# The MLP's falling products with weights stationary: tokens move, sums are kept by features and turned at the end

## Reference

```
hid = square(relu(rms_norm(x, g_pre_mlp) @ w_up))      # w_up   1024 x 4096
y   = x + rms_norm(hid @ w_down, g_post_mlp)           # w_down 4096 x 1024
rms_norm(v, g) = v * rsqrt(mean(v*v over the features) + 1e-6) * g
```

## Time and profile before

| | |
|---|---|
| median of 3 runs | 2000.29 us (1996.58 to 2002.13) |
| the profiled execution, its own time | 2001.27 us |
| its span, first to last instruction | 1999.5 us |
| mean granted TensorE clock | 0.978 of full |
| busy: PE / PEld / DVE / ACT / POOL | 1911.2 / 1720.5 / 1154.8 / 712.1 / 584.6 us |
| first matmul of the MLP / last one ends | 1187.5 / 1976.7 us |
| rising products, 2304 matmuls, start to start | 23.91 us a chunk |
| falling products, 1728 matmuls, start to start | 25.27 us a chunk |

### The profile page before, as it was taken

One profiled execution on the slowest core, in us unless ns is written; L12 is line 12 of the kernel. 1 busy time (PEld: TensorE's weight loads), 2 busy tenths in 40 slices (PEclk: granted clock), 3 DMA queues, 4 the chain that ended last, 5 costly groups with the idle time before them and its releaser, 6 DMA issues. The chain is left out here.

```text
span 1999.5 us, 31095 instructions
## 1 busy us (share of the span) xinstructions
PE 1911.2 (96%) x11132; PEld 1720.5 (86%) x11132; DVE 1154.8 (58%) x2651; ACT 712.1 (36%) x1420; POOL 584.6 (29%) x445
## 2 busy tenths in 40 slices
PE   5999999999999999999988979999999999999995
PEld 5889999877779999999987858888888888888884
DVE  5249999998645666676755653333333333333337
ACT  4335544233334555555644331122211221112212
POOL 2316544234223334343311012222222222222224
PEclk9999999999988999999998989999999999999998
DMA  5423333333446444443214321111111111111204
GB/s 169 130 67 91 94 98 90 87 100 97 103 121 140 97 97 97 97 97 86 66 27 158 121 95 43 43 43 46 42 42 42 43 46 42 42 42 42 63 0 158
DMA packets 180393, 160.18 MB, mean 80 GB/s; under 512 B 101472, under 2 KB 148432, under 8 KB 180288
## 3 DMA queue, kind: packets, MB, share of 16 engines
q1 hardware_dynamic: 166144, 140.32, 25.0%
q10 hardware_dynamic: 14144, 18.49, 4.0%
HBM read 120.63 MB, written 39.27 MB: 80 GB/s over the span
## 5 line engine op out<-in xcount | busy, mean ns | idle before, releaser
L2142 PE MATMUL ps<-x2T_hi,weights 128*128 128x362 f32 (+1 forms) x1536 | 383.5, 329 | 5.3 <-DVE weights L2108 5.3
L2160 PE MATMUL ps<-weights,hid_hi 128*128 128x512 f32 (+1 forms) x1152 | 363.0, 396 | 0.0
L2142 PEld LDWEIGHTS ps<-x2T_hi,weights 128*128 128x128 f32 x1536 | 273.7, 189 | 7.0 <-DVE weights L2108 5.5
L2093 DVE TENSOR_TENSOR total<-total,ps 128x512 f32<-128x512 f32 (+1 forms) x270 | 184.8, 686 | 164.3 <-PE ps L2160 163.4
L2160 PEld LDWEIGHTS ps<-weights,hid_hi 128*128 128x128 f32 (+1 forms) x1152 | 209.6, 182 | 57.1
L2142 PE MATMUL ps<-x2T_lo,weights 128*128 128x362 f32 (+1 forms) x768 | 253.0, 329 | 0.0
L976 PE MATMUL ps<-xT_hi,w 128*128 128x362 f32 (+1 forms) x960 | 246.1, 331 | 1.6 <-PEq L160 1.6
L2078 DVE TENSOR_TENSOR hidden<-hidden 128x362 f32<-128x362 f32 (+1 forms) x96 | 51.6, 537 | 311.3 <-ACT hidden L2051 311.3
L2160 PE MATMUL ps<-weights,hid_lo 128*128 128x512 f32 (+1 forms) x576 | 228.1, 396 | 0.0
L2011 POOL TENSOR_TENSOR weights<-down_raw,weights 128x512 fp32r<-128x512 f32 x64 | 82.8, 1294 | 419.9 <-ACT weights L2042 419.9
L951 DVE MATCH_REPLACE8 score<-top,score 128x1024 f32<-128x1024 f32 (+5 forms) x208 | 198.8, 961 | 0.0
(11 more groups left out here) (187 smaller groups left out, 3225.5 us busy)
## 6 DMA issues: line engine op xcount, KB each, us to landing
q_raw<-q_scr SPq DMA_DIRECT2D x80, 256.0 KB, 5.1
w_raw<-in_w_in ACTq DMA_DIRECT2D x64, 256.0 KB, 3.0
up_raw<-in_w_up SPq DMA_DIRECT2D x64, 256.0 KB, 2.8
down_raw<-in_w_down SPq DMA_DIRECT2D x64, 256.0 KB, 2.6
gates<-gate_scr SPq DMA_DIRECT2D x34, 256.0 KB, 4.6
x_in<-in_x_prompt SPq DMA_DIRECT2D x16, 512.0 KB, 4.8
gate_scr<-stage SPq DMA_DIRECT2D x32, 256.0 KB, 3.1
q_scr<-stage SPq DMA_DIRECT2D x40, 181.0 KB, 3.1
```

Of the source, the lines that this page charges most:

```text
L2093: dve.tensor_tensor(out, out, ps[:r, UP_BANKS + g % DOWN_BANKS, :], ALU.add).then_inc(added, 1)
L2142: last = pe.matmul(ps[:, g % UP_BANKS, 0:n], a[:, k, fs], b, start=(k == 0 and i == 0), stop=(k == KT - 1 and i == 2))
L2160: last = pe.matmul(ps[:r, UP_BANKS + g % DOWN_BANKS, :], a, b[:, f, cols], start=(f == 0 and i == 0), stop=(f == FT - 1 and i == 2))
```

## The change

The falling products swap their operands. A 128 x 128 slice of `w_down` is stationary, and the hidden values of a token block (364 or 362 tokens) move. The groups are (feature tile o of 8, token block b of 3), block by block: 24 a chunk, of 6 matmuls. The result, and so `total`, has output features on the partitions: `[P, KT, N_QUERY]`. VectorE adds 24 pieces of 364 or 362 columns a chunk. The norm runs over the features and the output is stored by tokens, so each token tile is transposed at the end: 8 transposes of 128 x 128 into two PSUM banks (`turn_total`). ScalarE squares and VectorE scales out of these banks, into `y`, three buffers, where GpSimd adds the residual and SP stores from.

The last chunk is now written out after the loop. Tiles 0 to 3 are transposed during it, after groups 10, 14, 18 and 22, into banks 0 and 1, and scaled by VectorE after its additions 11, 15, 19 and 23; tiles 4 to 8 after the last group (tiles 4 and 8 in banks 0 and 1, tiles 5, 6, 7 in banks 2 to 7). A tile that reuses banks waits for the scaling of the tile before in them; a scaling from tile 3 on waits for the store of three tiles before.

```diff
@@ -1916,7 +1916,9 @@
...
     UP_GROUPS = [(f, t0, n) for f in range(FT) for t0, n in TOK_BLOCKS]
-    DOWN_GROUPS = [(t, half) for t in range(TILES) for half in range(2)]
+    DOWN_GROUPS = [(o, b) for b in range(len(TOK_BLOCKS)) for o in range(KT)]
+    BLOCK_END = [t0 + n for t0, n in TOK_BLOCKS]
+    PER_BLOCK = KT
     N_UP, N_DOWN = len(UP_GROUPS), len(DOWN_GROUPS)
@@ -1932,7 +1934,8 @@
...
         hid_lo = sb("hid_lo", [P, FT, N_QUERY], F32R)
-        total = sb("total", [P, TILES, D])
+        total = sb("total", [P, KT, N_QUERY])
+        y = sb("y", [P, 3, D])
         x1_in = sb("x1_in", [P, 2, D])
@@ -1946,12 +1949,29 @@
...
         sq_done, std_ready, rstd_ready, refined = sem("p5_sq_done"), sem("p5_std_ready"), sem("p5_rstd_ready"), sem("p5_refined")
-        scaled, y_ready, y_stored = sem("p5_scaled"), sem("p5_y_ready"), sem("p5_y_stored")
+        y_turned = sem("p5_y_turned")
+        scaled, y_ready, y_stored = sem("p5_scaled"), sem("p5_y_ready"), [sem(f"p5_y_stored{i}") for i in range(3)]
...
         FIRST_BY_DVE = range(1, KT, 2)
+        def whole_after(t):
+            return PER_BLOCK * (1 + min(b for b, end in enumerate(BLOCK_END) if t * P + tile_rows(t) <= end))
+        LAST_BANKS = [0 if whole_after(t) < N_DOWN or t == SAMPLE_TILE else 2 * (t % 4) for t in range(TILES)]
+        TURNED_AT = [PER_BLOCK + 2, PER_BLOCK + 6, 2 * PER_BLOCK + 2, 2 * PER_BLOCK + 6] + [N_DOWN] * (TILES - 4)
+        SCALED_AT = [at + 1 if at < N_DOWN else at for at in TURNED_AT]
+        def y_banks(t):
+            return ps[:tile_rows(t), LAST_BANKS[t]:LAST_BANKS[t] + 2, :].rearrange("p b n -> p (b n)")
+        def banks_used_before(t):
+            return max((s for s in range(t) if LAST_BANKS[s] == LAST_BANKS[t]), default=None)
@@ -1959,7 +1979,7 @@
...
                 dst = y_prompt[0, toks(t), :] if t < SAMPLE_TILE else y_sample[0]
-                sp.dma_start(dst, total[:r, t, :]).then_inc(y_stored, 16)
+                sp.dma_start(dst, y[:r, t % 3, :]).then_inc(y_stored[t % 3], 16)
@@ -1993,7 +2013,8 @@
...
                 store_y(sp, TILES - 1)
-                sp.wait_ge(y_stored, 16 * TILES)
+                for i in range(3):
+                    sp.wait_ge(y_stored[i], 16 * (TILES // 3))
@@ -2020,7 +2041,7 @@
...
                     pool.wait_ge(x1_loaded[t % 2], 16 * (t // 2 + 1))
-                    pool.tensor_tensor(total[:r, t, :], total[:r, t, :], x1_in[:r, t % 2, :], ALU.add).then_inc(y_ready, 1)
+                    pool.tensor_tensor(y[:r, t % 3, :], y[:r, t % 3, :], x1_in[:r, t % 2, :], ALU.add).then_inc(y_ready, 1)
                     pool.wait_ge(y_ready, t + 1)
@@ -2061,8 +2082,8 @@
...
                     r = tile_rows(t)
-                    act.wait_ge(added, (N_CH - 1) * N_DOWN + 2 * t + 2)
-                    act.activation(squares[:r], total[:r, t, :], ACT.Square, accum_out=col["sum_sq"][:r, t:t + 1]).then_inc(sq_done, 1)
+                    act.wait_ge(y_turned, t + 1)
+                    act.activation(squares[:r], y_banks(t), ACT.Square, accum_out=col["sum_sq"][:r, t:t + 1]).then_inc(sq_done, 1)
                     act.wait_ge(sq_done, t + 1)
@@ -2083,14 +2104,14 @@
...
                 def add_down(j, g, first=False):
-                    t, half = DOWN_GROUPS[g]
-                    r = tile_rows(t)
-                    out = total[:r, t, 512 * half:512 * half + 512]
+                    o, b = DOWN_GROUPS[g]
+                    t0, n = TOK_BLOCKS[b]
+                    out, more = total[:, o, t0:t0 + n], ps[:, UP_BANKS + g % DOWN_BANKS, 0:n]
                     dve.wait_ge(down_done, j * N_DOWN + (g + 1))
                     if first:
-                        dve.tensor_copy(out, ps[:r, UP_BANKS + g % DOWN_BANKS, :]).then_inc(added, 1)
+                        dve.tensor_copy(out, more).then_inc(added, 1)
                         return
-                    dve.tensor_tensor(out, out, ps[:r, UP_BANKS + g % DOWN_BANKS, :], ALU.add).then_inc(added, 1)
+                    dve.tensor_tensor(out, out, more, ALU.add).then_inc(added, 1)
@@ -2100,7 +2121,9 @@
...
                     refine_rstd(dve, refined, 3 * t, one("rstd"), one("rstd_0"), one("mean_sq"), one("newton"))
-                    dve.scalar_tensor_tensor(out=total[:r, t, :], in0=total[:r, t, :], scalar=one("rstd"), in1=gain[:r, :],
+                    if t >= 3:
+                        dve.wait_ge(y_stored[t % 3], 16 * (t // 3))
+                    dve.scalar_tensor_tensor(out=y[:r, t % 3, :], in0=y_banks(t), scalar=one("rstd"), in1=gain[:r, :],
                                              op0=ALU.mult, op1=ALU.mult).then_inc(scaled, 1)
@@ -2118,17 +2141,18 @@
...
                 dve.wait_ge(gain_loaded, 16)
+                for g in range(N_DOWN):
+                    add_down(N_CH - 1, g)
+                    for t in range(TILES):
+                        if g == SCALED_AT[t]:
+                            scale_total(t)
                 for t in range(TILES):
-                    add_down(N_CH - 1, 2 * t)
-                    add_down(N_CH - 1, 2 * t + 1)
-                    if t >= 2:
-                        scale_total(t - 2)
-                scale_total(TILES - 2)
-                scale_total(TILES - 1)
+                    if SCALED_AT[t] >= N_DOWN:
+                        scale_total(t)
...
             def _(pe):
-                def chunk(j, first=False):
+                def chunk(j, first=False, final=False):
                     pe.wait_ge(up_lo_done, (j + 1) * KT)
@@ -2143,27 +2167,43 @@
...
                     pe.wait_ge(down_lo_done, (j + 1) * DOWN_UNITS)
-                    for g, (t, half) in enumerate(DOWN_GROUPS):
-                        r = tile_rows(t)
-                        block_of = max(b for b, (t0, n) in enumerate(TOK_BLOCKS) if t0 < t * P + r)
-                        if half == 0:
-                            pe.wait_ge(hid_lo_done, j * N_UP + (len(TOK_BLOCKS) * (FT - 1) + block_of + 1))
+                    for g, (o, b) in enumerate(DOWN_GROUPS):
+                        t0, n = TOK_BLOCKS[b]
+                        if o == 0:
+                            pe.wait_ge(hid_lo_done, j * N_UP + (len(TOK_BLOCKS) * (FT - 1) + b + 1))
                         if g >= DOWN_BANKS:
...
                             pe.wait_ge(added, (j - 1) * N_DOWN + (N_DOWN - DOWN_BANKS + g + 1))
-                        cols = slice(512 * half, 512 * half + 512)
+                        cols = slice(o * P, (o + 1) * P)
                         for f in range(FT):
-                            h_hi, h_lo = hid_hi[:, f, toks(t)], hid_lo[:, f, toks(t)]
-                            for i, (a, b) in enumerate(((h_hi, down_hi), (h_hi, down_lo), (h_lo, down_hi))):
-                                last = pe.matmul(ps[:r, UP_BANKS + g % DOWN_BANKS, :], a, b[:, f, cols],
+                            h_hi, h_lo = hid_hi[:, f, t0:t0 + n], hid_lo[:, f, t0:t0 + n]
+                            for i, (a, h) in enumerate(((down_hi, h_hi), (down_hi, h_lo), (down_lo, h_hi))):
+                                more = pe.matmul(ps[:, UP_BANKS + g % DOWN_BANKS, 0:n], a[:, f, cols], h,
                                                  start=(f == 0 and i == 0), stop=(f == FT - 1 and i == 2))
-                        last.then_inc(down_done, 1)
+                        more.then_inc(down_done, 1)
+                        for t in range(TILES):
+                            if final and TURNED_AT[t] == g:
+                                turn_total(t)
+                def turn_total(t):
+                    r = tile_rows(t)
+                    if LAST_BANKS[t] == 0:
+                        pe.wait_ge(relu_done, N_CH * N_UP)
+                    pe.wait_ge(added, (N_CH - 1) * N_DOWN + whole_after(t))
+                    if banks_used_before(t) is not None:
+                        pe.wait_ge(scaled, banks_used_before(t) + 1)
+                    for o in range(KT):
+                        turned = pe.transpose(y_banks(t)[:, o * P:(o + 1) * P], total[:, o, toks(t)], c["ident"][:])
+                    turned.then_inc(y_turned, 1)
                 chunk(0, first=True)
-                with pe.Fori(1, N_CH) as j:
+                with pe.Fori(1, N_CH - 1) as j:
                     chunk(j)
+                chunk(N_CH - 1, final=True)
+                for t in range(TILES):
+                    if TURNED_AT[t] >= N_DOWN:
+                        turn_total(t)
```

## The result

The changed kernel takes 1979.55 us (median of 4, 1977.99 to 1982.4) against 2000.02 us: a ratio of 0.990, interval 0.9885 to 0.9915, so 17 to 23 us faster. Forecast were 1988.0 us and at best 1983.0. Run again beside the kernel before it was 0.9903 (0.9886 to 0.9919), 19.4 us.

The account below looks back on a forecast made before the run. The MLP was taken as bound by TensorE's matmuls in sequence, then a 22.8 us tail. -21.8 (falling) + 3.5 (transposes) + 5.7 (tail) = -12.6 us gave 1988.7, as a median 1988.0 us; range 1983.0 to 1996.5.

Parts of the forecast that it names:

- Falling stretches: Falling products of 16 MLP chunks: 144 matmuls at 166.0 ns, 23.91 us for 25.27 a chunk, gain 21.8 us.
- Rising stretches: The MLP's 144 rising products a chunk, 23.91 us, 166.0 ns each; no change counted in the sum.
- Rival A: Falling matmul's extra time belongs to its place, not width: 171.8 ns, gain only 8.5 us, 2001 us; chance 0.14.
- Rival D: Weight loads bound the matmul pitch at this width; time is the forecast's; chance inside the forecast's 0.68.
- Additions: VectorE's partial sums: 24 of about 531 ns a chunk for 18 of 687, hidden behind TensorE, cost zero.
- The written-out last chunk: Last MLP chunk written out behind the loop: cost zero, as the first chunk already hands over without delay.
- Transposes in the last chunk: Tiles 0 to 3 turned between groups 10 and 23: 0.87 x 4 = 3.5 us on TensorE's path, none waiting.
- margin at turn 1: Last falling stretch: scale 0 ends at 15.6 us, turn 1 comes at 15.8; slack 0.2 us.
- Rival C: Turns 1 to 3 each wait a microsecond for the scale before, TensorE stands: +3 us, 1991; chance 0.11.
- Tail: After the last product's end T: last scale at T + 22.7 for T + 17.0, 3.81 us a tile, loss 5.7 us.
- Rival B: Tail not held by line 78, GpSimd's 2.34 + 0.14 the period: 5.3 us less, 1982.7 us; chance 0.07.

Follow-up runs that it names:

- 256-column run: The kernel before with its falling products in quarters of 256 columns in place of halves of 512, 216 matmuls a chunk; ratio 1.0007 (0.9997 to 1.0017).

## Why the prediction was off, step by step

- **Falling stretches.** The failed term. "I take 23.91 us for a falling stretch" was mis-sized: 23.59. Reading the price off the rising products was right in kind (24 groups in sequence, no gap, no new wait), but 166.0 ns was one level of several, and I took it for the shape's own. 163.8 against 166.0 ns is 0.32 us a stretch, 5.1 us in 16. My bounds came from means of other places and ended at 164.5; single blocks run at 160.0. That such levels exist and shift with the layout is shown; what picks them is not.
- **Rising stretches.** The second term that failed, put at nothing because untouched: they lost 0.15 us each, all in one group of six, 2.4 us with the first stretch. (0.2 of this is the first, which lies anywhere from 25.5 to 26.5 us in the runs' profiles and is no effect of the change.)
- **Rival A** is refuted by the falling stretch itself (163.8 ns for its 171.8) and by the 256-column run. Its "for" (three 512-column places 7 ns apart) I read as an argument about one theory, when it was the width of an uncertainty in both directions. What makes those 7 ns no run shows: 64 bytes moved that pitch by 0.9 ns only.
- **Rival D** gave the forecast's time, so the time doesn't test it; its mechanism is refuted by the pitch of 117.3 ns with a load to each matmul.
- **Additions** at 532 ns for 531, hidden. **The written-out last chunk** costs nothing. Both as said.
- **Transposes in the last chunk**: 27.63 - 23.59 = 4.0 us for 3.5. The four took 0.87, 1.06, 0.99 and 1.00. No turn waited. The margin at turn 1 was as thin as said: scale 0 ended at 1935.29 and the turn began at 1935.44, 0.15 us later for 0.2. Rival C did not occur, but did when the turns were moved (waits of 0.88 to 1.05 us).
- **Tail**: last scale at 1970.31, T + 22.9, for T + 22.7. Turn 4 waited for scale 3 (2.89 us) and then took 1.08 us; the granted clock was 1.00 from 1949.9 to 1954.0, so the slower turn that I allowed for did not come. Line 78 held each later tile, the stores did not bind. Rival B is refuted here, and its mechanism shown by the run that changed line 78.
- **Sum.** -26.9 (16 x 1.68) - 2.4 + 4.0 + 5.9 = -19.4 us, inside the 17 to 23 measured. With the forecast's 166.0 and untouched rising products it is -11.9. The range's lower end, 1983.0, held 3.5 us for the pitch and nothing for the rising products; the two gave 7.5.

## What to carry to other kernels

A matmul was paid here by the columns that move, 117 ns for 256, 164 for 362, 234 for 512, whatever the stationary side held: put the ragged dimension on the moving side, where it is paid by the column (here 5.6% of the falling columns), and not on the stationary side, where a tile of 64 tokens cost as much as one of 128 (231.7 against 234.0 ns a matmul of 512 columns in the kernel before). A pitch read from the trace was good to about 2% for a stretch (23.36 to 23.84 us) and 4% for a block (160.0 to 166.7 ns) in other buffers of the same shape, and to 0.6% for code that wasn't touched, so give a sum over thousands of matmuls that width in both directions. Before adding a buffer, look at what stands ahead of its load in the queue that issues it.

## What the runs showed of the hardware

At 362 columns and a granted clock of 1.00 TensorE's pitch has levels from 160.0 to 166.7 ns in long even runs. They repeat over executions on four chips to a hundredth of a microsecond a stretch (23.59 and 23.76 us), are the same with and without relu's zeros in the hidden values, and shift when buffers move by 64 bytes (23.84) or another order of blocks precedes (rising 23.91). The lowest is still 9.2 ns over columns / 2.4 GHz. What picks the level is open.

A one-column product of two SBUF tensors on VectorE took 1.84 us beside GpSimd's addition and 0.16 without it; the same product with a pointer scalar took 0.21 beside it, and a scale that reads PSUM its usual 1.28.
